# A wait for the first gather of token rows ahead of the up loads of the first expert pair (layer 0)

## The reference, cut to what matters

```python
def expert_choice_ffn(h, w_router, w_gate, w_up, w_down):
    cap = EC_CAPACITY_FACTOR * T // N_EXPERTS
    aff = jax.nn.softmax(jnp.einsum('btd,de->bte', h, w_router), axis=-1)
    gate, idx = lax.top_k(jnp.swapaxes(aff, 1, 2), cap)
    xs = jax.vmap(lambda hb, ib: hb[ib])(h, idx)
    hid = jax.nn.silu(jnp.einsum('becd,edf->becf', xs, w_gate)) * jnp.einsum('becd,edf->becf', xs, w_up)
    y = jnp.einsum('becf,efd->becd', hid, w_down) * gate[..., None]
    return jax.vmap(lambda yb, ib: jnp.zeros((T, D)).at[ib.reshape(-1)].add(yb.reshape(-1, D)))(y, idx)
```

## Time and profile before

| what | value |
|---|---|
| median of 3 runs | 1759.9 us (1759.55 to 1762.53) |
| time of the profiled execution | 1758.64 us |
| span of that execution, first to last instruction | 1756.8 us |
| PE (TensorE matmul) busy | 1668.0 us, 95% of the span |
| DVE, ACT, POOL busy | 651.4, 452.4, 417.2 us |
| mean granted TensorE clock | 0.98 |

### The profile page before, as it was taken

One profiled execution on the slowest core, in us unless ns is written; L12 is line 12 of the kernel. 1 busy time (PEld: TensorE's weight loads), 2 busy tenths in 40 slices (PEclk: granted clock), 3 DMA queues, 4 the chain that ended last, 5 costly groups with the idle time before them and its releaser, 6 DMA issues.

```text
span 1756.8 us, 34615 instructions
## 1 busy us (share of the span) xinstructions
PE 1668.0 (95%) x14265; PEld 1033.3 (59%) x14265; DVE 651.4 (37%) x1391; ACT 452.4 (26%) x1013; POOL 417.2 (24%) x558
## 2 busy tenths in 40 slices
PE   6999999889999998999999999999978999999998
PEld 4565555567886565555555445555568955454544
DVE  4145334345544141112211424524446634323233
ACT  4211423253433021111111231243354222111011
POOL 2713102416660003111111141300537700000000
PEclk9999999999999988999999999999999999999999
DMA  9520000058884256999998511100041033899995
GB/s 328 149 96 24 1 25 17 13 163 283 264 264 170 70 193 226 357 356 359 360 350 317 179 37 60 49 0 17 13 124 29 15 120 145 320 413 413 406 414 234
DMA packets 160350, 323.65 MB, mean 184 GB/s; under 512 B 30152, under 2 KB 118126, under 8 KB 144878
## 3 DMA queue, kind: packets, MB, share of 16 engines
q1 hardware_dynamic: 127584, 287.20, 44.1%
q0 software_dynamic: 7008, 21.74, 4.6%
q10 hardware_dynamic: 25646, 13.12, 2.7%
HBM read 307.31 MB, written 14.71 MB: 183 GB/s over the span
## 4 chain that ended last, share of the span: by engine, by line
PE 51%; DVE 3%; issue 3%; DMA 2%; POOL 2%; SPq 1%; ACT 1%; ACTq 0%; DVEq 0%; POOLq 0%
PE psum L1314 12%; PE psum L703 8%; PE psum L1345 6%; PE psum L1323 4%; PE psum L1395 3%; PE psum L1166 3%; PE psum L1357 2%; PE psum L856 1%; PE psum L835 1%; DMA big<-in_moe_w_down 1%; PE psum L1419 1%; SPq L1563 1%; PE psum L728 1%; PE psum L1399 1%; PE psum L1336 1%
## 5 line engine op out<-in xcount | busy, mean ns | idle before, releaser
L703 PE MATMUL psum<-hT,ring 128*128 128x512 f32 (+3 forms) x880 | 298.3, 496 | 0.0
L703 PEld LDWEIGHTS psum<-hT,ring 128*128 128x128 f32 (+1 forms) x880 | 165.3, 190 | 121.1 <-issue 110.8
L1314 PE MATMUL psum<-ring,arena 128*64 128x256 f32 x1536 | 174.5, 384 | 9.6 <-DVE xT L2770 3.6
L1314 PEld LDWEIGHTS psum<-ring,arena 128*64 128x64 f32 x1536 | 109.2, 138 | 72.1 <-issue 18.8
L1166 PE MATMUL psum<-hT,ring 128*128 128x512 f32 (+1 forms) x384 | 140.2, 522 | 0.9 <-DVE xT L2624 0.9
L2741 DVE TENSOR_TENSOR arena<-arena,psum 128x384 f32<-128x384 f32 (+1 forms) x32 | 15.6, 488 | 261.6 <-PE psum L1323 162.5
L1166 PEld LDWEIGHTS psum<-hT,ring 128*128 128x128 f32 x384 | 72.4, 190 | 64.6 <-issue 61.3
L3125 POOL DMA_INDIRECT big<-h_rows_lat,idx x16 | 15.7, 984 | 375.2 <-PE psum L1419 173.9
L2770 DVE SCALAR_TENSOR_TENSOR xT<-psum,modraw,xT 128x512 f32<-128x512 f32 (+1 forms) x136 | 79.7, 624 | 16.6 <-PE psum L1395 9.9
L835 PE MATMUL psum<-hT,ring 128*128 128x256 f32 (+1 forms) x192 | 81.5, 534 | 0.0
L2134 ACT COPY arena<-psum 128x512 f32<-128x512 f32 (+2 forms) x49 | 23.7, 484 | 214.5 <-PE psum L1336 143.3
(11 more groups left out here) (409 smaller groups left out, 3132.6 us busy)
## 6 DMA issues: line engine op xcount, KB each, us to landing
ring<-in_moe_w_gate SPq DMA_DIRECT2D x64, 1024.0 KB, 9.6
ring<-in_ada_w SPq DMA_DIRECT2D x48, 1024.0 KB, 7.0
ring<-in_moe_w_up SPq DMA_DIRECT2D x32, 1024.0 KB, 10.9
hT<-in_moe_w_down SPq DMA_DIRECT2D x24, 1024.0 KB
ring<-in_w_in SPq DMA_DIRECT2D x20, 1024.0 KB, 5.3
big<-in_moe_w_up SPq DMA_DIRECT2D x16, 1024.0 KB
sz<-in_moe_w_down SPq DMA_DIRECT2D x16, 1024.0 KB
big<-in_moe_w_down SPq DMA_DIRECT2D x16, 1024.0 KB
```

What stands on the lines that cost most here:

```text
L703: m = pe.matmul(b[0:c1 - c0, 0:n], lhsT=w[:, k, c0:c1], rhs=hT[:, k, t0:t0 + n], start=k == 0, stop=k == KD - 1)
L1314: m = pe.matmul(b[e * CAP_L:(e + 1) * CAP_L, 0:2 * P], lhsT=xs[:, k, e, 0:CAP_L], rhs=w[e][:, 2 * (k - ks[0]) + q, :], start=k == 0, stop= ...
```

## The change

Between the last gate load (part 3) and the first of the two up loads (part 4) of the first pair of layer 0, SP waits until `gath` is 32, that is until both gathers of the first pair have landed. Nothing else is edited. Layer 1 has no such wait.

```diff
                 for m in range(SLOTS - LENT, SLOTS):
                     slot_free(n + m)
+                    if l == 0 and m == SLOTS - 2:
+                        sp.wait_ge(sems[l]["gath"], 16 * 2)
                     part_of_pair(n + m, l, 0, m)
```

## The result

The changed kernel takes 1752.16 us (median of 5 runs, 1746.97 to 1756.06) against 1760.03 us of the kernel before (5 runs, 1759.55 to 1762.56). The ratio is 0.9947, 95% interval 0.9928 to 0.9965: faster by 9.3 us, 6.2 to 12.7 (the medians alone differ by 7.9). The forecast was 6.9 us. Pooled, the 29 runs of the changed kernel from these three comparisons and 102 of the kernel before (timed beside the experiments up to after_c, with before_b) have means of 1751.6 and 1760.0 us and standard deviations of 4.2 and 3.3 us; the difference is 8.4 us with a standard error of 0.84 (the root of 4.18^2/29 + 3.33^2/102), so 6.7 to 10.0 us. The forecast 6.9 lies in that interval, near its lower end.

The account below looks back on a forecast made before the run. TensorE, busy 1668.0 of 1756.8 us, was taken as the bound, standing 3.75 us for the first context gather. Terms 3.7 + 1.6 + 1.6 = 6.9 us off the 1759.9 median gave 1753.0 us, range 1750.8 to 1757.5.

Parts of the forecast that it names:

- The gathers wait behind the ups' bytes: First pair's gathers, layer 0: without the ups queued ahead they land 4.8 and 4.7 us after issue, context at 665.9.
- TensorE's filler is the next limit, so 3.7 us and not 4.9: Ahead of the transposes: filler holds TensorE until 667.05, so 3.7 us gained though the gather is 4.9 us earlier.
- The transposes at the full clock, 1.6 us: Four banks of transposes behind the first gather: 2.56 us at full clock instead of 4.17, gaining 1.6 us.
- The third term: First 48 gate products: 5.40 us instead of 7.03 if the clock holds over the 1.8 us stand, gaining 1.6 us.
- forecast A: Whole kernel: all three gains come, 6.9 us less, 1753.0 us; chance 0.55.
- rival B: Between transposes and gate products the clock falls; gain 5.3 to 3.6 us, time 1754.6 to 1756.3; chance 0.20.
- second and third term: Full clock in the transposes and in the first 48 gate products, 1.6 us gained in each.
- the one microsecond allowed below the sum: Lower end of the forecast range: 1750.8 us, a us of spread below the other reference, 1751.7.
- No cost from the late ups: Up loads issued near 666 land near 673, with 9 us to spare before TensorE's up products, so hidden.
- The second pair's gathers: Issued at about 670 beside the ups, they may take 9 us instead of 4.8, at no cost.

Follow-up runs that it names:

- after_c: The changed kernel again, unchanged, for a third profile and more times; ratio 0.9960 (0.9942 to 0.9979) against the kernel before.
- before_b: The kernel before, unchanged, for a second profile and more times; ratio 0.9999 (0.9983 to 1.0014) against the kernel before.
- half: The changed kernel with the wait one entry later, so one up load goes ahead of the gathers and one behind; ratio 0.9977 against the kernel before.
- idx: The changed kernel with SP's wait on the indices instead of the gathers' landing; ratio 0.9994 against the kernel before.
- filler: The kernel before, without the wait, with 11 filler products instead of 7 ahead of the gather's transposes; ratio 0.9992 against the kernel before.
- nofill: The changed kernel without the 7 filler products ahead of the gather's transposes; ratio 0.9982 against the kernel before.
- late: The changed kernel with the ups waiting for the pair's gate products instead of the gathers; ratio 1.0030 against the kernel before.
- five: The changed kernel with 5 filler products instead of 7 ahead of the gather's transposes; ratio 0.9962 against the kernel before.

## Why the prediction was right, and where it was off

**The gathers wait behind the ups' bytes: right.** Forecast was a landing after 4.8 and 4.7 us, measured were 5.0 and 4.6. It is shown by the dose (half) and by idx, where the ups are later but still ahead and nothing is gained. One reading beside it was wrong: the queues don't share "half and half" from 664 us on the earlier trace rows. While both have work it is two bytes to one for queue 1 (last section); the even sum comes from the last microsecond, when queue 1 has run out.

**TensorE's filler is the next limit, so 3.7 us and not 4.9: right.** The stand of 3.75 us became none. From the filler's start to the first transpose it is 12.4 us in the three profiles of the kernel before and 8.5 in the four of the changed kernel, on average. With five products of filler TensorE came to the landed rows 1 us sooner.

**The transposes at the full clock, 1.6 us: right**, 2.55 us in all four profiles, and 2.6 in filler, where the gather is as late as before. That this was a matter of transposes coming right behind dense products is seen in nofill, where they ran at 0.50. The Trainium skill (TensorE: Matmul & The Clock Gate, section "PE-mode transpose") would have it that the full clock doesn't engage in transposes. The traces agree only in part. The row 670.70:673.30 has 1.00 kept over 16 of them. In the kernel before the grant rose from 0.50 to 1.00 at about 642.5 us, while nothing but the transposes of L1245 ran. But the 16 transposes of nofill did not raise it in 4.1 us.

**The third term, the clock held over the stand, 1.6 us: right in three profiles, wrong in one.** It is not one value. The first, second and fourth profile of the changed kernel, and late, kept the clock (5.4 us for the 48 products), after_c lost it (8.4 us). In filler and five the grant fell within the gate products (7.1 us). So forecast A and rival B both happen, execution by execution, and the average of the four profiles is 1.0 us.

**The step that failed: the size of the clock's part, and the one microsecond allowed below the sum.** The prediction put its second and third term at 3.2 us together, each at one value, looked at the low clock only from 670 to 680 us, and let the range end one microsecond below the sum. The runs showed a larger part and a wider scatter. Over all runs the mean granted clock goes from 0.9801 to 0.9838, which is 70.0 and 56.7 us at the low clock (2 x (1 - clock) x span). 13.3 us less are worth at most 6.6 us. With the 3.7 us of the stand the gain may thus be up to 10.3 us, and 8.4 was measured. The clock's part is then 8.4 - 3.7 = 4.7 us (3.0 to 6.3), where 3.2 were forecast. A straight line through the times of these 131 runs against their granted clock, with one step between the two kernels, says much the same: at an equal clock the changed kernel is 3.1 us faster (standard error 0.5), and 5.2 us go with the clock. The 3.2 is still inside the interval, so that the term is too small is likely, not proven.

**The range.** The three runs of the kernel before that were on record lay within 3 us. But single executions scatter with a standard deviation of 3.3 and, changed, of 4.2 us. Most of it goes with TensorE's clock: taken off by a straight line against the granted clock, 1.8 us are left of the 3.3. A comparison of five runs each came out 2.4 us beyond the sum. Its ratio times 1760.03 gives 1750.7, just below the bound of 1750.8. Part of that is chance: the pooled 8.4 us would give 1751.6, inside the range.

**No cost from the late ups: right.** They landed 6.0 us after issue, at about 676, and TensorE took them up at 686.05, so 10 us ahead; 9 were forecast. The second pair's gathers, for which up to 9 us were allowed, took 6.2 and 6.1.

**What stays open.** The middle of the four profiles is 6.8 us shorter on average (44.8 for 51.6): 0.4 ahead of the filler, 3.9 from there to the transposes, 1.6 in them, 1.0 in the gate products (the parts are rounded). That this equals the forecast sum is luck, since the third term was 0.6 smaller and others made up for it. In the 0.4 TensorE waits for nothing that the change moves. The runs say 8.4 with a standard error of 0.84. Whether the rest is chance in which executions were profiled, or a place that these profiles don't show, isn't settled. The low clock in the neighbourhood fell by 12.5 us: some 8.5 of it lie behind the first transpose, where the kernel before has 10.2 us in each of three profiles, and the rest ahead of it. Nor is it known what decides whether the clock falls at the stand: filling the stand changed no mean.

## What to carry to other kernels

A prefetch that is issued a moment ahead of a transfer on the critical path delays it by its own bytes, even from another engine's queue; if the prefetch has slack, let it wait for the landing. A wait that ended 0.4 us ahead of the transfer's issue gained nothing here. Price such a change by the stand that it removes and by the clock behind the stand: here the second was about as large as the first. And take the spread of single executions from many runs before giving a narrow range; three runs that agree prove little.

## What the runs showed of the hardware

In these kernels the queue that had its loads in the engines kept the newcomer out at first, and only then did the two share. In idx the latent gather is issued at 658.58, but from 660 to 662 us queue 1 has 99.9% of the engines and the gathers' queue nothing; from 662 to 664 it has 18.9%. In the kernel before the gathers' queue first moves bytes in the stretch from 664 us on, 4 us after the issue at 659.82, against under 2 us for the second pair's gathers. The queues of the kernel before from 664 to 667 us (packets, MB, share):

```profile
q1 hardware_dynamic: 100, 0.80, 63.2%
q0 software_dynamic: 105, 0.43, 34.8%
```

The Trainium skill (DMA: Bandwidth & Descriptors, section "Queues, rings and completion order") says that each engine goes round the queues that have work for it, packet by packet. The sharing from 664 us on agrees: as many packets from one queue as from the other. It isn't an equal share of bytes, since a packet of queue 1 held 8 KB here and one of the gathers 4 KB. The 2 us before it don't show it.

The same instructions ahead of the edit took 627.9 to 637.1 us in the fifteen profiles of this study, with the low clock at different places: the profile after has 6.8 us of it between 330 and 340 us, the first of the kernel before none there. That is more than the whole effect studied here. A comparison by one span each would have found 2.8 us or, with after_c, the wrong sign (1759.3 for 1756.8).
